# Two activation tiles of a two-block kernel change places in on-chip memory

## The reference

```python
# first_block: layer 0 with the recurrent mixer, layer 1 with the sparse attention
x = x + rglru_mixer(rms_norm(x, g_mix0), ...)
x = x + square(relu(rms_norm(x, g_mlp0) @ w_up0)) @ w_down0      # 1024 -> 4096 -> 1024
x = x + dsa_mixer(rms_norm(x, g_mix1), ...)                      # latent attention, top 64 keys
x = x + square(relu(rms_norm(x, g_mlp1) @ w_up1)) @ w_down1
x = rms_norm(x, g_final)
# second_block: modulation by a condition, one wide projection, three branches, a gated merge
z  = h @ w_in                        # 1024 -> 8704
m  = ga*(ya @ w_out_a) + gb*(yb @ w_out_b) + gc*(yc @ w_out_c)
out = x + gate * (m @ w_o)
```

## Time and profile before

| | |
|---|---|
| median of 3 runs | 931.14 us |
| the profiled execution, its own time | 930.94 us |
| its span (first to last instruction) | 929.3 us |
| PE busy with matmuls | 888.5 us, 96% |
| weight loads (PEld) | 844.3 us, 91% |
| DVE busy | 706.7 us, 76% |
| ACT busy | 443.3 us, 48% |
| POOL busy | 204.0 us, 22% |
| mean granted TensorE clock | 0.99 of full speed |

### The profile page before, as it was taken

The page is one execution under the profiler, slowest core; times in us unless marked ns, Lnnn a source line. Parts: engine busy times, 40 slices in busy tenths (PEclk is TensorE's granted clock), DMA queues, the critical chain, the costliest instruction groups (busy, mean ns, idle before and its releaser), DMA issues.

```text
span 929.3 us, 17949 instructions
## 1 busy us (share of the span) xinstructions
PE 888.5 (96%) x6992; PEld 844.3 (91%) x6992; DVE 706.7 (76%) x1076; ACT 443.3 (48%) x636; POOL 204.0 (22%) x220
## 2 busy tenths in 40 slices
PE   7998999999999997899999999998999999999998
PEld 5997899999999985599999999988899999899998
DVE  4767788898777688677666677686658998996793
ACT  7672244443444346745444444343357646543741
POOL 5221332233421000032222222141204213110000
PEclk9999999999999997999999999999999999999999
DMA  9753566678898532045555656554535454455442
GB/s 347 225 204 109 190 250 222 224 249 253 243 280 233 164 109 90 2 154 190 181 184 183 196 184 188 170 175 162 162 131 200 145 165 148 136 181 181 158 161 91
DMA packets 46960, 167.86 MB, mean 181 GB/s; under 512 B 5776, under 2 KB 5920, under 8 KB 46640
## 3 DMA queue, kind: packets, MB, share of 16 engines
q1 hardware_dynamic: 40896, 146.82, 47.3%
q0 software_dynamic: 5856, 20.00, 7.7%
q10 hardware_dynamic: 144, 0.15, 0.1%
HBM read 165.50 MB, written 1.44 MB: 180 GB/s over the span
## 4 chain that ended last, share of the span: by engine, by line
PE 66%; DVE 22%; issue 5%; ACT 4%; DMA 1%; DVEq 0%; ACTq 0%; POOL 0%; SPq 0%
PE bank L565 18%; PE bank L567 18%; PE bank L566 17%; DVE wlo L1305 7%; PE bank L629 5%; ACT whi L968 2%; DVE ada_prod L1478 2%; DVE ada_prod L1454 2%; PE bank L647 2%; DVE xl L1324 1%; PE bank L789 1%; DVE tq L1509 1%; DMA raw<-weights 1%; PE bank L883 1%; DVE score L1586 1%
## 5 line engine op out<-in xcount | busy, mean ns | idle before, releaser
L1305 DVE TENSOR_TENSOR wlo<-raw,whi 128x1024 fp32r<-128x1024 f32 x260 | 325.6, 1284 | 93.3 <-ACT whi L968 92.1
L565 PE MATMUL bank<-xh,whi 128*128 128x256 f32 x1328 | 381.4, 287 | 9.4 <-DVE vv L1724 3.4
L566 PE MATMUL bank<-xl,whi 128*128 128x256 f32 x1328 | 376.3, 283 | 0.0
L567 PE MATMUL bank<-xh,wlo 128*128 128x256 f32 x1328 | 376.2, 283 | 0.0
L968 ACT ACTIVATE whi<-raw 128x1024 fp32r<-128x1024 f32 x260 | 266.3, 1051 | 123.5 <-PE bank L567 107.0
L565 PEld LDWEIGHTS bank<-xh,whi 128*128 128x128 f32 x1328 | 255.2, 192 | 20.7 <-issue 9.5
L566 PEld LDWEIGHTS bank<-xl,whi 128*128 128x128 f32 x1328 | 255.4, 192 | 0.2
L567 PEld LDWEIGHTS bank<-xh,wlo 128*128 128x128 f32 x1328 | 255.3, 192 | 0.0
L565 PE MATMUL bank<-hhi,whi 128*128 128x256 f32 x512 | 143.8, 281 | 3.2 <-DVE wlo L1305 3.2
L567 PE MATMUL bank<-hhi,wlo 128*128 128x256 f32 x512 | 142.9, 279 | 0.0
L566 PE MATMUL bank<-hlo,whi 128*128 128x256 f32 x512 | 142.8, 279 | 0.0
(11 more groups left out here) (278 smaller groups left out, 1079.4 us busy)
## 6 DMA issues: line engine op xcount, KB each, us to landing
raw<-weights SPq DMA_DIRECT2D x260, 512.0 KB, 4.4
ada_raw<-ada_w POOLq DMA_DIRECT2D x24, 512.0 KB, 4.5
plain<-plain_w SPq DMA_DIRECT2D x16, 512.0 KB, 6.7
relB<-rel_scratch POOLq DMA_DIRECT2D x8, 256.0 KB, 7.5
bl<-rpb_in POOLq DMA_DIRECT2D x32, 64.0 KB, 3.4
x<-x_in SPq DMA_DIRECT2D x4, 256.0 KB, 6.1
cond<-cond_in POOLq DMA_DIRECT2D x1, 1024.0 KB, 7.3
cx<-ctx_in POOLq DMA_DIRECT2D x1, 1024.0 KB, 7.8
```

Source lines behind the costliest of these rows:

```text
L565: mmul(dst, hi, rh, start=start, stop=False)
L566: mmul(dst, hi, rlo, start=False, stop=False)
L567: return mmul(dst, lo, rh, start=False, stop=stop)
L1305: V_.tensor_tensor(wlo[:, sl], raw[:, sl], whi[:, sl].bitcast(F32), ALU.subtract)\
```

## The change

The two lines that allocate `xh` and `xl` move from behind `x` to behind `hcl`. No instruction is added, removed or moved; only addresses in instructions differ.

```diff
         x = sb("x", [P, DT, S])
-        xh = sb("xh", [P, 12, S], F32R)
-        xl = sb("xl", [P, 12, S], F32R)
         cols = sb("cols", [P, NCOLS])
         ones = sb("ones", [P, P])
...
             cond = sb("cond", [P, 2, D], F32, room)
         hch = sb("hch", [P, DT, S], F32R)
         hcl = sb("hcl", [P, DT, S], F32R)
+        xh = sb("xh", [P, 12, S], F32R)
+        xl = sb("xl", [P, 12, S], F32R)
```

## The result

The changed kernel takes **921.4 us** (median of 19 runs, 916.61 to 933.06), beside 932.82 us for the kernel before on the same chips (19 runs, 930.24 to 937.37). The ratio is 0.9892, 95% interval 0.9868 to 0.9917: faster by 1.1%, about twice the forecast gain, and outside the range, whose low end was 923.5. The 19 runs are no single heap: ten lie from 916.6 to 921.4 us, eight from 925.4 to 929.4, one above. The profiled execution, 921.22 us with a span of 919.5, is of the lower group. The median is the tenth of the 19 and the slowest of the lower group; the next run up, 925.4 us, lies inside the range. So it is how the runs divide that puts the result outside. What the two groups are turned out to be the heart of the case.

The account below looks back on a forecast made before the run. PE's `acc3` matmuls were taken to bound 312.8 us of the chain. Terms -5.8 + 0.4 + 0.25 = -5.15 us gave 925.8 us for the profiled execution, 926.0 for the median; range 923.5 to 928.3.

Parts of the forecast that it names:

- Which stretches follow PE: Six stretches where the chain of waits runs through `acc3` matmuls, 312.8 us, 108 of 166 `xh` chunks: -5.8 us.
- 0.4 and 0.25: Losses taken off the gain: +0.4 us for DVE holding the pace in ca to bz, +0.25 us for stage v.
- up0 hides a faster PE: In up0 DVE and ACT are slower, so its 32 chunks (1.7 us) give nothing and PE waits longer.
- Each `xh` matmul falls from 120.0 to 117.8 ns: All `xh` chunks at the new offset: 1.85% faster, -5.8 us on the chain.
- down1 stays unchanged: down1, with `hhi` and `hlo` as moving operands, was to keep 2.827 us a chunk, no gain.
- The offset decides: The moving operand's offset above a multiple of 1024 sets its speed, 704 being faster than 128: chance 0.80, around 926.0 us.
- The stage v: There `xh` is stationary: 48 matmuls slow from 226.7 to about 233 ns, +0.25 us.
- Tiles that move down: `hch`, `hcl` and other tiles move 24576 bytes down but keep their offset: cost 0, other end +1.1 us.
- That nothing changes: Rival: address is not the cause of the 2.2 ns; gain 0, 931.1 us, chance 0.09.
- The region: Rival: low memory is slow, whatever the offset; border near 98 KB 927.1 us (0.04), at 113 KB 930.3 us (0.03).
- Collisions of DVE and POOL: Rival: POOL's mask additions overlap weight splits, 1.1 us each, up to 932.6 us; chance 0.04 with unseen causes.

Follow-up runs that it names:

- after_c: Further profiled execution of the unedited changed kernel, from the group above 924 us: up1 and down1 at 117.8 ns a matmul, together 213.22 us.
- after: First profiled execution of the changed kernel, from the lower group: 921.22 us, up1 and down1 at 113.3 ns a matmul.
- bench2: No model, PE streams matmul triples alone, moving operand shifted against weights in 16-byte steps; 64 bytes repeated eight times behind waits: five at 113.3 ns, three at 117.8.
- e3: Weight slots and `x` moved along, so weights and all moving operands lie 704 above a multiple of 1024: 935.34 us, ratio 1.004 to the kernel before.
- e6: Changed kernel with `whi` and `wlo` shifted 208 bytes, so moving operands start 112 past the weights modulo 256: 935.94 us, ratio 1.0025 to the kernel before.
- bench4: No model, single chunks at eight weight places and sixteen moving places: 112 bytes apart is good with weights on multiples of 32, 118 to 120 ns at odd 16s.
- e4: Kernel before with `hch`, `hcl` brought behind `x` to offset 128, like weights, `xh` and `xl`: one run of 936.06 us.
- bench1: No model, PE alone streams matmul triples, moving operand at multiples of 64 bytes: 113.3 to 120.0 ns a matmul, period 256 bytes.
- e1: `xh`, `xl` at offset 704 but low (88768 and 101056), `hch`, `hcl` at their old places: 922.58 us, ratio 0.9887 to the kernel before.
- after_d: Further profiled execution of the unedited changed kernel, from the group below 922 us: up1 and down1 at 113.3 ns a matmul, together 206.60 us.

## Why the prediction was wrong, and where it was right

**Which stretches follow PE: right.** The shares of the chain of the earlier trace rows handed on what PE gained. after_c had the forecast spacing and so tests them. up1 to down1 is 1.63 us shorter (1.65 forecast), down1 to k as long as before, gates to out_a 1.33 shorter (24 chunks x 0.0533 = 1.28). From k to gates it is 1.49 shorter, and the working had 40 chunks x 0.0533 = 2.13 less 0.4 and 0.25, 1.48; that these agree is luck. The part from ca to gates is 2.35 us shorter in all six profiles, with the eight chunks named above at 113.3 ns in it, and after_c lost 0.85 in k, where its clock was at 0.5 for 6.8 us (3.4 in before). The start is 1.3 us later with its lower clock, up0 to up1 0.6 us longer, so that the span of after_c is 3.0 us shorter in all and not 5.15.

**up0 hides a faster PE: right.** It takes 94.8 us in after and 95.7 in after_c, where before took 95.6, and PE's wait on `wlo` there grew from 0.3 to 2.2 us, by the waits of the changed kernel from 107 to 202 us:

```profile
PE bank L565 <- DVE wlo L1305: 2.2, 5, 0.8
```

**"Each `xh` matmul falls from 120.0 to 117.8 ns": this step failed.** It took the distance-64 spacing of the tiles shown in the earlier trace rows for the only one. The runs show two, 117.8 and 113.3, settled at waits of PE. With 113.3 in up1 the term there is 32 x 0.16, about 5 us, not 1.7; and because the outcome holds on past the end of up1, the sentence that down1 stays unchanged failed with it (-3.4). In the upper group, 8 of the 19 runs with 925.4 to 929.4 us, the forecast spacing did come in up1, by the two profiles of that group. The second spacing was in the trace of before, and neither a term nor the range used it. Its timeline of PE in down0, the starts of two successive chunks:

```profile
244.57 0.28 PE L565 MATMUL bank<-hhi,whi 128*128 128x256 f32 x1
...
247.29 0.28 PE L565 MATMUL bank<-hhi,whi 128*128 128x256 f32 x1
```

2.72 us for a chunk of `hhi`, where a chunk of down1 takes 2.827; three chunks in a row, from 241.7 to 250.2 us, stand at 113.3 ns. With `xh` at distance 0 up1 ran at 120.0, and down1, which follows it without a wait, came out at 117.8, as the streams placed without a wait in bench2 did. The change made a second outcome possible in up1, and behind it in down1; it did not only lower a constant. A range with a case for it, both stages at 113.3, would have reached 926.0 - 6.6 = 919.4.

**"The offset decides" was right only in the sign.** The offset of the moving tile modulo 1024 was taken as the cause. e3 shows that `hhi` and `hch` lose their 117.8 at that very offset when the weights lie alike, and the bench that the period is 256 bytes, measured from the weights, with a say of the weights' own place (e6, bench4). For this change both readings forecast the same sign, which is why the result alone could not tell them apart.

**The stage v: right.** The timeline of PE there:

```profile
651.33 0.39 PE L843 MATMUL bank<-whi,xh 128*128 128x512 f32 x1
...
654.13 0.39 PE L843 MATMUL bank<-whi,xh 128*128 128x512 f32 x1
```

12 matmuls in 2.80 us, 233.3 ns each, where the earlier trace rows had 226.7 for `xh`: a place that helps as moving operand costs a little as stationary one. What counts is again the relation: in e3 and e4, where `hch` lies like the weights, the stage cv falls from 233.4 to 227.1 ns.

**Tiles that move down: right.** att_out kept 117.8 ns. **The rivals.** That nothing changes is refuted: at a clock of 1.00 the same matmul starts every 113.3, 117.8 or 120.0 ns, by the bytes at which its two operands lie and, at distance 64, by what was settled at the last wait. The Trainium skill (SBUF — State Buffer, "Who interferes with whom") has TensorE's two read ports as independent; whether they meet there or elsewhere no run shows, but that the places of the two operands do not matter to each other, as the rival took from it, is not so here. That no other engine makes PE wait for a port is not contradicted: bench1 has the same spacings with PE alone at work. The Trainium skill (TensorE: Matmul & The Clock Gate, "Wait — 56ns, not 53.3ns?") has N / 2.4 + 2.5 ns for back-to-back matmuls, measured at 128 and 512 columns; the estimate from it for 256 is 109.2 ns, and no stream here went below 113.3. The region fell with e1. Collisions of DVE and POOL cost nothing that shows: DVE's busy time is 705.5 us beside 706.7, and ca to bz came out shorter, not longer.

## What to carry to other kernels

Where PE sets the pace with back-to-back matmuls, compare the start-to-start spacing of stages with the same form; differences of a few per cent at a full clock may lie in where the two operands start relative to each other, and shifting one of them by some tens of bytes is a cheap trial (here 1.4% with one pair of tiles moved, 2.2% with three). Not every shift helps: e6 had the same distance with the weights elsewhere and gained nothing. Look at the whole distribution of that spacing, not at the value of one stage: a rare value in the profile of before can become the common one after. And when runs of one kernel fall into two groups, profile an execution of each before explaining the median.

## What had not been expected of the hardware

One sequence of instructions on the same bytes has two speeds, 113.3 and 117.8 ns a matmul, chosen at a wait of PE and kept until the next, over 62 chunks (169 us) in the changed kernel; with PE alone at work it shows as well. What picks the one or the other at the wait is open: in bench2 the waits before fast and slow streams look the same (0.26 us). That some stretches come out alike in all six profiles speaks for the exact timing at the wait and against pure chance, but no run varied it. Why the weights' own place changes what distance 112 is worth is open too; the table shows that it does. Not settled is also the lower clock near 85 us in five of six profiles of the changed kernel: PE's wait ahead of it is as long in after_d, which kept 1.00.
